# Hybrid block with PEER experts: expert numbers of gathered tiles 1 and 2 computed 32 product groups ahead of their dots

## The reference

```python
s1, i1 = lax.top_k(sc[:, :, 0], 16)          # 8 heads, two halves of the key
s2, i2 = lax.top_k(sc[:, :, 1], 16)
cand = (s1[..., :, None] + s2[..., None, :]).reshape(t, 8, 256)
top_s, top_p = lax.top_k(cand, 16)
e1 = jnp.take_along_axis(i1, top_p // 16, axis=-1)
e2 = jnp.take_along_axis(i2, top_p % 16, axis=-1)
experts = (e1 * 128 + e2).reshape(t, 128)
gates = jax.nn.softmax(top_s, axis=-1).reshape(t, 128)
pre = jnp.einsum('td,tkd->tk', x, u_tab[experts])
act = jax.nn.gelu(pre) * gates
y = jnp.einsum('tk,tkd->td', act, v_tab[experts])
```

## Time and profile before

| | us |
|---|---|
| median of 3 runs | 3052.64 (3042.54 to 3055.24) |
| the profiled execution, device time | 3044.79 |
| its span, first to last instruction | 3043.0 |
| products of the up stage, first to last start | 932.7 to 2050.0 |
| TensorE busy in the span | 2759.7 (91%) |
| VectorE busy | 2355.4 (77%) |
| GpSimd busy | 1435.0 (47%) |
| ScalarE busy | 1256.3 (41%) |

### The profile page before, as it was taken

One profiled execution on the slowest core, in us unless ns is written; L12 is line 12 of the kernel. 1 busy time (PEld: TensorE's weight loads), 2 busy tenths in 40 slices (PEclk: granted clock), 3 DMA queues, 4 the chain that ended last, 5 costly groups with the idle time before them and its releaser, 6 DMA issues. The chain is left out here.

```text
span 3043.0 us, 40193 instructions
## 1 busy us (share of the span) xinstructions
PE 2759.7 (91%) x15003; PEld 2410.1 (79%) x15003; DVE 2355.4 (77%) x4166; ACT 1256.3 (41%) x2507; POOL 1435.0 (47%) x1118
## 2 busy tenths in 40 slices
PE   7998799879998889999999999991999999999996
PEld 6776566339998889999999999981887877878885
DVE  3375586234976999798898978866999999999997
ACT  3244333012222247878877778841222222222222
POOL 1121310002855585555545555533666666666763
PEclk9999798989999999999999999995999999999998
DMA  4110100212103489999989899979999999999996
GB/s 115 42 35 25 45 1 21 69 42 56 32 26 100 157 291 328 351 341 345 356 319 368 319 352 362 359 301 350 385 376 372 380 373 375 376 376 383 386 386 238
DMA packets 315442, 754.28 MB, mean 248 GB/s; under 512 B 22944, under 2 KB 141728, under 8 KB 312688
## 3 DMA queue, kind: packets, MB, share of 16 engines
q0 software_dynamic: 111104, 403.02, 35.6%
q1 hardware_dynamic: 203088, 344.50, 32.0%
q10 hardware_dynamic: 1056, 4.19, 0.3%
HBM read 659.35 MB, written 92.27 MB: 247 GB/s over the span
## 5 line engine op out<-in xcount | busy, mean ns | idle before, releaser
L1815 POOL DMA_INDIRECT v_rows<-in_peer_v,row_numbers x384 | 597.8, 1557 | 381.8 <-DVE y L1879 257.2
L1608 POOL DMA_INDIRECT u_rows<-in_peer_u,row_numbers x384 | 539.4, 1405 | 433.9 <-DVE row_weights L1712 376.7
L1510 PE MATMUL expert_pre<-h2T,uT_hi 128*128 128x320 f32 x4096 | 679.3, 315 | 59.0 <-DVE uT_lo L1695 30.8
L1510 PEld LDWEIGHTS expert_pre<-h2T,uT_hi 128*128 128x128 f32 x4096 | 621.1, 191 | 64.2 <-DVE uT_lo L1695 34.2
L1921 PE MATMUL expert_out<-v_hi,w_hi 128*128 128x512 f32 x1280 | 502.7, 393 | 85.4 <-DVE w_lo L1858 85.3
L1879 DVE SCALAR_TENSOR_TENSOR y<-v_rows,row_weights,y 128x1024 f32<-128x1024 f32 x384 | 488.9, 1279 | 60.3 <-DMA v_rows<-in_peer_v,row_numbers 42.8
L1921 PE MATMUL expert_out<-v_lo,w_hi 128*128 128x512 f32 x1280 | 501.0, 391 | 0.0
L1921 PE MATMUL expert_out<-v_hi,w_lo 128*128 128x512 f32 x1280 | 500.7, 391 | 0.0
L1712 DVE CUSTOM_DVE_ANT_0 u_rows<-u_rows,h_rows_kept 128x1024 f32<-128x1024 f32 x384 | 464.6, 1237 | 5.5 <-DMA u_rows<-in_peer_u,row_numbers 5.5
L1921 PEld LDWEIGHTS expert_out<-v_hi,w_hi 128*128 128x128 f32 x1280 | 241.9, 189 | 142.3 <-DVE w_lo L1858 91.9
L1839 ACT ACTIVATE w_hi<-acts_times_gates 128x640 fp32r<-128x640 f32 x128 | 94.8, 741 | 604.7 <-DVE acts_times_gates L1851 604.5
(11 more groups left out here) (301 smaller groups left out, 4226.2 us busy)
## 6 DMA issues: line engine op xcount, KB each, us to landing
u_chunk<-in_peer_u_turned SPq DMA_DIRECT2D x128, 512.0 KB, 6.9
v_chunk<-in_peer_v SPq DMA_DIRECT2D x128, 512.0 KB, 9.5
acts_dram<-expert_acts SPq DMA_DIRECT2D x128, 320.0 KB, 5.0
gates_dram<-pick_memory SPq DMA_DIRECT2D x20, 2048.0 KB, 10.9
acts_times_gates<-acts_dram SPq DMA_DIRECT2D x128, 320.0 KB, 10.7
gates_group<-gates_dram SPq DMA_DIRECT2D x32, 1280.0 KB, 18.5
w_in_columns<-in_w_in SPq DMA_DIRECT2D x20, 512.0 KB, 3.9
wq_tile<-in_peer_wq SPq DMA_DIRECT2D x16, 512.0 KB, 4.1
```

The lines of the kernel that those rows point to most:

```text
L1510: last = nc.tensor.matmul(pre[:, (2 * c + half) % 4, 0:WIDTH], part[:, c % 2, k], m.h2T[:, t, k, HALVES[half]], start=n == 0, stop=n == le ...
L1608: pool.indirect_dma_start(rows[:, k % RING], None, d.peer_u, bass.IndirectOffsetOnAxis(ap=m.row_of[:, f, slot:slot + 1], axis=0)).then_inc ...
L1815: pool.indirect_dma_start(rows[:, k % ROW_RING], None, d.peer_v, bass.IndirectOffsetOnAxis(ap=m.row_of[:, f, slot:slot + 1], axis=0)).then ...
```

## The change

Tiles 1 and 2 leave the list of tiles whose keys are made at the beginning. Their key steps begin 32 quarters ahead of the quarter in which their own first dot is due: with the new pace at quarter 173 for tile 1 and 324 for tile 2. The order of the tiles becomes 0, 3, 4, 1, 5, 6, 2, 7 (beginnings 40, 48, 104, 173, 187, 269, 324, 351). The dots are spread over quarters 54 to 508 instead of 58 to 508, so the first is emitted at quarter 55 and the first fetch at quarter 49. The assertion only states that no two tiles' steps overlap.

```diff
@@ experts_up
-    DOTS_FROM, DOTS_TO = 58, QUARTERS - 4
+    DOTS_FROM, DOTS_TO = 54, QUARTERS - 4
...
-    early = [0, F] + [t for t in range(1, F)]
+    ROWS_AHEAD = 32
+    early = [0, F]
     keys_from = {t: KEYS_FROM + 8 * n for n, t in enumerate(early)}
+    for t in range(1, F):
+        keys_from[t] = DOTS_FROM + P * t * (DOTS_TO - DOTS_FROM) // DOTS - ROWS_AHEAD
     for t in range(F + 1, NT):
         keys_from[t] = max(SPREAD_FROM + ((t - F) * GROUPS - 24) * (SPREAD_TO - SPREAD_FROM) // ALL,
                            KEYS_FROM + 8 * len(early))
     order = sorted(range(NT), key=lambda t: keys_from[t])
+    assert all(keys_from[b] - keys_from[a] >= KEY_STEPS + 1 for a, b in zip(order, order[1:]))
```

## The result

The changed kernel takes 3058.97 us (median of 22 runs, 3042.71 to 3072.43), the kernel before 3047.38 (22 runs, 3037.09 to 3066.87). The ratio is 1.0034, with a 95% interval from 1.0019 to 1.0050: about 10 us slower, within the 0.5% that was called no difference. Measured a second time, beside the last three experiments, it was 1.0036 (1.0022 to 1.0049). The forecast was +4.1 us.

The account below looks back on a forecast made before the run. TensorE bounds the up stage, waiting for low halves from VectorE and GpSimd. A front gain of 10.7 us and a middle cost of 14.8 give +4.1; against the 3052.6 median, 3057 us, range 3042 to 3072.

Parts of the forecast that it names:

- What bounds the kernel: Up stage: TensorE is the bound, its products waiting 59.0 us for low halves, 30.8 on VectorE's and 28.3 on GpSimd's.
- The signs named beforehand: Changed profile: a gap of about 6 us before chunk 14, chunk 22 at about 1106, two new middle gaps of 4 to 6.
- Parts (a) to (d), the front: Up to chunk 22: tiles 1 and 2's keys leave, dots and fetches come 4 quarters sooner; a gain of 10.7 us.
- Part (c), the new stall of chunk 14: GpSimd's queue: fetch 0 now stands ahead of chunk 14's low half, so TensorE stalls 6.2 us.
- Fetch 6's wait: GpSimd's queue: fetch 6 waits for the first dot 2.2 us, in place of 7.57.
- Part (d), GpSimd's pace: Behind that, GpSimd sets the pace: a low half and 3.38 fetches take 8.07 us per chunk, above TensorE's 7.04.
- Part (e), the price of a block: Middle of the up stage: each tile's key steps cost 7.4 us, so tiles 1 and 2 cost 14.8 us.
- slow start: After a long TensorE gap: slow matmuls add 2.8 us, as chunk 16's second half began 6.34 us behind its first, not 3.52.
- The neighbour: Rival: tile 1's keys lie 14 quarters from tile 5's, whose cost rises by 5.8 us, giving 3063 us; chance 0.09.
- The sum: Whole kernel: minus 10.7 plus 14.8 us is +4.1, forecast 3057 us, no difference that can be told.
- A front that gives nothing: Rival: up to chunk 22 the front stays GpSimd-bound and gains nothing; 3068 to 3070 us, chance 0.20.
- A free middle: Rival: VectorE's idle 137.7 us absorbs the moved keys' 28.4, leaving only the gain; 3042 or 3035 us, chance 0.08.

Follow-up runs that it names:

- the last three experiments: Three follow-up kernels measured on the same chip beside the changed kernel's second profile, which itself had ratio 1.0036 to the kernel before.
- the keys at 155: Changed kernel with tile 1's keys beginning at quarter 155 and tile 2's at 311 instead of 173 and 324; one run, no ratio.
- those 48 ahead: Changed kernel with the keys of tiles 1 and 2 48 quarters ahead instead of 32; ratio 1.0020 to the kernel before.
- tiles 1 and 2 stretched: Changed kernel with tiles 1 and 2 doing one key step in five quarters, beginning at 147 and 308; ratio 0.9963 to the kernel before.
- all stretched with the dots from 54: Changed kernel with key steps of tiles 4, 1, 5, 6, 2, 7 one in five quarters, dots from quarter 54; ratio 0.9943 to the kernel before.
- the kernel without blocks: Changed kernel without the key steps of tiles 1 and 2, their row numbers made from tile 0's digits; ratio 0.9979 to the kernel before.

## Why the prediction was right, and where its terms were off

**What bounds the kernel** held: what differs between the profiles of the up stage are gaps of TensorE released by low halves, and slow matmuls behind them. The signs named beforehand came: GpSimd's part of the idle time down to 17.8 (some 20 had been said), VectorE's up to 44.5 (about 42), chunk 22 at 1102.9 when the offset is added (1106), no gap over 3 us between chunks 14 and 22. The new gaps of the middle, said to be 4 to 6 us, came at 6.58 and 5.44. That the forecast time of 3057 us lies only 2 us beside the measured 3059 is luck: it was counted from a median of three runs, 3052.6, that 22 runs put at 3047.4, and this error of 5 and the 6 us that the sum was short cancel out.

**Parts (a) to (d), the front**: a gain of 10.7 us forecast. Six profiles share the changed front and have their keys in full: at chunk 24 they gave 13.8, 12.7, 11.6, 10.1, 10.0 and 10.0 (the two of the change, the keys at 155, those 48 ahead, tiles 1 and 2 stretched, all stretched with the dots from 54), a mean of 11.4. By time, the kernel without blocks is only 6 us ahead, with 2 to 11 in its interval. Both hold the 10.7.

**Part (c), the new stall of chunk 14**: 6.2 us forecast, 5.17 measured. It was a little smaller because four fetches took 7.6 us (1024.25 to 1031.81), not 9.8, of which the low half behind them took 1.1 back (3.57 us, not 2.5). Fetch 6's wait: 2.2 forecast, 1.92 measured. What I had not drawn from it is that the four quarters sooner are a loss. With the keys in front they cost 8 us (3 to 12). With the keys moved they cost 6 in each of two pairs (1.0034 against 1.0015, 0.9943 against 0.9923; in the second the keys stand in the same quarters), neither clear of noise alone, and in all of them chunk 14 is 7 us later than with 58.

**Part (d), GpSimd's pace**: a cycle of 8.07 us forecast. Chunk 15's low half starts at 1043.24 and chunk 22's at 1097.68, 7.8 us per chunk. The step held, and so did its price: the 24 fetches between the two take 1.28 us on average, forecast 1.33. The Trainium skill, page "SBUF — State Buffer", section "Who interferes with whom", says that a VectorE instruction with two SBUF inputs contends with a GpSimd one that reads SBUF. By that rule the trace agrees in the first fetch, which ran beside a comparison and a product of tile 3's keys and took 2.89 us; it does not in the fetch at 1030.87, beside a comparison that had begun 0.02 us before it, which took 0.94.

**Part (e), the price of a block, was the term that was mis-sized.** Forecast 7.4 us each, 14.8 in all. By times of many runs it is 17 us for two (changed against no blocks), with 10 to 23 in its interval, so by this pair alone 14.8 would stand. The other figures point above it: the two profiles of the change lose 23.0 and 26.2 from chunk 32 to 94, and spreading the two blocks saved 22 (16 to 29). What the ledger shows for tiles 1 and 5, 12.1 us from chunk 32 to 58, can be added up from the trace: tile 1's block leaves gaps of 1.04, 6.58 and 1.32 us, tile 5's gap is 1.0 larger, and a slow start costs 2.8 (the prediction's figure), 12.7 in all. Tile 2's is 0.54, 1.03, 5.44 and 2.8, so 9.8, with 9.9 and 12.3 in the ledger from 74 to 94.

So three things were mis-sized. The neighbour: tile 5's gap grew, by 1.0 us against before and by 1.2 against the kernels without a block near it. The main gap of tile 1 is itself 6.58 and not 5.80. And the small gaps beside the main ones (1.04 and 1.32; 0.54 and 1.03) were left out; the quiet window against which tiles 5 and 6 were read, 1370 to 1420, is not free of one itself, in TensorE's timeline of the kernel before:

```profile
1404.05 2.61 PE L1510 MATMUL expert_pre<-h2T,uT_hi 128*128 128x320 f32 x16 [1.08 <-DVE uT_lo L1695]
```

The slow start behind a long gap was in the 7.4 already, as the products of a window are fewer by it too. (Tile 7's 7.7 is 7.5 at the 5.7 products per us named; that moves the mean by 0.05.) The neighbour I had as a rival, with 0.09 and +5.8 us, and it should have stood in the sum as a part, with some 1 us.

**The sum**: +4.1 forecast, +10 measured. By times it is made of -6 and +17. By the ledger it is made of -13.8 and +23.0 in the first profile, +9.2 at chunk 94 and +10.9 at the stage's end, and of -12.7 and +26.2 in the second. The other 2.2 us of the 13.1 by which the spans differ lie outside the up stage. The two accounts agree that the front's term had its sign and about its size and that the blocks' was the one too small, and leave open some 5 to 8 us in each.

**The rivals.** A front that gives nothing did not come. A free middle did not come, but its idea, that VectorE has the idle time for 28 us of keys, was half right: it has, or nearly, for keys that are spread out.

## What to carry to other kernels

Work that is moved out of a crowded place into a place where its engine has idle time on average still costs what it is late by at its first deadline: ask how far that engine may fall behind there, and put the work in pieces smaller than that. Here the same 28 us cost 17 us (10 to 23) as two bursts and nothing that the times show when spread over five times as many slots. And when two edits come together, try each alone: the dots sooner looked like part of the gain and were a loss of 6 to 8 us.

## What the runs showed of the hardware

In the up stage a gap of over 5 us in TensorE's work is followed by slow matmuls, mostly 4.63 us for 16 instead of 2.51 (3.91 was the least), where a gap of 1.45 us is not (2.03 us for 12 at 1045.83); in between both happen: 3.45 us before chunk 15 left 2.03 for 12 in the kernel before, and 3.57 for 12 in the kernel with the keys moved alone. With the keys 48 quarters ahead even a gap of 2.12 us, before 1449.20, was followed by 3.57 for 12; the granted clock was 1.00 in the window before that gap, 1440 to 1446, and 0.51 behind it, 1449.2 to 1452. The windows of line 1514 of the changed kernel (length, busy TensorE and weight loads, granted clock, DMA share, GB/s): the end of tile 1's gap and the matmuls behind it, then 50 us with tile 1's slow start and tile 5's gap, then the 50 us behind them:

```profile
1306.00:1315.00 9.00, 5.30 (x20) 5.30 (x21) 0.50 0.61 202
...
1310.00:1360.00 50.00, 37.81 (x212) 36.00 (x212) 0.84 0.78 272
1360.00:1410.00 50.00, 43.22 (x282) 41.07 (x280) 1.00 0.91 344
```

The granted clock of the first is 0.50 of full speed, the lower level of 1.2 GHz; that of the second is 0.84, a mean over stretches at either level, and that of the third 1.00, the upper level of 2.4 GHz.
